# Ends of sub-layers in an encoder trunk: normalisation by quarters, three bank pairs for the transposes, and a first unit whose low part GpSimd makes

## The reference

```
for i in range(DEPTH):
    shift, scale, gate = _ada(c, ada_w[i, 0], ada_b[i, 0])
    h = x * (1.0 + scale) + shift
    y = _mixer_ab(h, ...) if i % 2 == 0 else _mixer_c(h, ...)
    x = _layer_norm(ALPHA * x + (1.0 + gate) * y, ln_g[i, 0], ln_b[i, 0])
    shift, scale, gate = _ada(c, ada_w[i, 1], ada_b[i, 1])
    h = x * (1.0 + scale) + shift
    y = _swiglu(h, ffn_w_in[i], ffn_w_out[i])
    x = _layer_norm(ALPHA * x + (1.0 + gate) * y, ln_g[i, 1], ln_b[i, 1])
```

## Time and profile before

| what | value |
|---|---|
| median of 3 runs (lowest, highest) | 2828.54 us (2824.93, 2829.81) |
| the profiled execution: its own time, its span | 2825.97 us, 2824.2 us |
| PE, DVE, ACT, POOL busy | 93%, 70%, 41%, 10% of the span |
| L477, the low parts of weights on DVE | 396 instructions, 2324 ns each |
| L472, the high parts on ACT | 396 instructions, 1915 ns each |
| L845, the power on GpSimd | 4 instructions, 947 ns each |
| mean granted clock of TensorE | 0.977 |

### The profile page before, as it was taken

The page is one execution under the profiler, slowest core; times in us unless marked ns, Lnnn a source line. Parts: engine busy times, 40 slices in busy tenths (PEclk is TensorE's granted clock), DMA queues, the critical chain, the costliest instruction groups (busy, mean ns, idle before and its releaser), DMA issues. The chain is left out here.

```text
span 2824.2 us, 42978 instructions
## 1 busy us (share of the span) xinstructions
PE 2636.7 (93%) x18094; PEld 2195.5 (78%) x18094; DVE 1973.2 (70%) x1838; ACT 1148.6 (41%) x1319; POOL 282.9 (10%) x199
## 2 busy tenths in 40 slices
PE   1999979998999999999999779999999999999996
PEld 1788869997777888888888567888778888888885
DVE  6778946776666888888887776765568755555557
ACT  1443336555434333333333335456343333333332
POOL 0000000000005000000000085541050000000000
PEclk9999979999999999999999899999999999999998
DMA  9899912220647888888887375654558755555552
GB/s 351 325 345 369 373 50 71 71 68 32 225 151 266 328 305 325 308 324 309 309 323 293 100 258 194 239 166 145 196 187 325 277 194 188 186 190 193 192 187 82
DMA packets 252881, 636.60 MB, mean 225 GB/s; under 512 B 10222, under 2 KB 17060, under 8 KB 230596
## 3 DMA queue, kind: packets, MB, share of 16 engines
q1 hardware_dynamic: 246578, 621.84, 61.4%
q10 hardware_dynamic: 6162, 12.72, 1.2%
HBM read 632.42 MB, written 2.10 MB: 225 GB/s over the span
## 5 line engine op out<-in xcount | busy, mean ns | idle before, releaser
L477 DVE TENSOR_TENSOR s_wl<-s_raw,s_wh 128x2048 fp32r<-128x2048 f32 x396 | 920.4, 2324 | 503.0 <-ACT s_wh L472 502.4
L472 ACT ACTIVATE s_wh<-s_raw 128x2048 fp32r<-128x2048 f32 x396 | 758.5, 1915 | 1168.4 <-PE pa L623 521.2
L621 PE MATMUL pa<-s_wh,s_hth 128*128 128x512 f32 x1616 | 644.5, 399 | 14.9 <-DVE s_wl L477 9.3
L622 PE MATMUL pa<-s_wl,s_hth 128*128 128x512 f32 x1616 | 633.9, 392 | 0.0
L623 PE MATMUL pa<-s_wh,s_htl 128*128 128x512 f32 x1616 | 633.8, 392 | 0.0
L621 PEld LDWEIGHTS pa<-s_wh,s_hth 128*128 128x128 f32 x1616 | 306.8, 190 | 88.8 <-issue 18.2
L623 PEld LDWEIGHTS pa<-s_wh,s_htl 128*128 128x128 f32 x1616 | 306.2, 189 | 65.5
L517 DVE SCALAR_TENSOR_TENSOR s_wide<-s_adaw,s_silu_c,s_wide 128x2048 f32<-128x2048 f32 x150 | 351.9, 2346 | 6.3 <-DMA s_adaw<-in_ada_w 6.3
L622 PEld LDWEIGHTS pa<-s_wl,s_hth 128*128 128x128 f32 x1616 | 306.9, 190 | 60.6
L621 PE MATMUL pb<-s_wh,s_hth 128*128 128x512 f32 (+1 forms) x816 | 319.1, 391 | 0.0
L622 PE MATMUL pb<-s_wl,s_hth 128*128 128x512 f32 (+1 forms) x816 | 318.5, 390 | 0.0
(11 more groups left out here) (361 smaller groups left out, 2562.1 us busy)
## 6 DMA issues: line engine op xcount, KB each, us to landing
s_raw<-in_ffn_w_in SPq DMA_DIRECT2D x176, 1024.0 KB, 5.2
s_adaw<-in_ada_w SPq DMA_DIRECT2D x160, 1024.0 KB, 6.3
s_raw<-in_ffn_w_out SPq DMA_DIRECT2D x88, 1024.0 KB, 7.4
s_raw<-in_ab_w_in SPq DMA_DIRECT2D x48, 1024.0 KB, 9.0
s_raw<-in_diff_w_in SPq DMA_DIRECT2D x48, 1024.0 KB, 5.1
s_raw<-in_ada_w SPq DMA_DIRECT2D x16, 1024.0 KB, 8.5
s_raw<-in_ab_w_out SPq DMA_DIRECT2D x16, 1024.0 KB, 5.5
s_qkv<-in_ada_w SPq DMA_DIRECT2D x16, 1024.0 KB, 7.3
```

The costliest lines, as they stand in the source:

```text
L472: act.activation(wh[:, s % 2, :, 0:width], raw[:, s, :, 0:width], ACT.Copy).then_inc(hi_done, 1)
L477: dve.tensor_tensor(wl[:, s % 2, :, 0:width], raw[:, s, :, 0:width], wh[:, s % 2, :, 0:width].bitcast(F32), ALU.subtract).then_inc(lo_done, 1)
L621: pe.matmul(o, a_hi, w_hi, start=start and k == 0, stop=False)
L622: pe.matmul(o, a_hi, w_lo, start=False, stop=False)
```

## The change

It has five parts, all in the three calls 1, 2 and 3.

1. `normal` works on a quarter of the columns (512) instead of a half (1024): quarters 0 and 1 before group 0, and 2 and 3 behind `lower(3)`.
2. The transposes use three bank pairs (`py`, `pb`, `pt`), so a group waits for the one three before it. Group 3 is moved from in front of unit 0 to between its first 12 and its second 12 matmuls (`mid`).
3. The units wait for their input group by group: k = 0 and 1 for the first of the two groups, k = 2 and 3 for the second.
4. The low part of unit 0's weights is made by GpSimd in two halves of 1024 columns (`low_first`), one in front of the power and one behind it; the first unit waits for these (`lo_first`) in place of `lo_done`. DVE no longer makes it, and raises `lo_done` for it behind `normal(3)`.
5. ACT no longer waits for `scaled(0)` before its first read of group 0.

```diff
+        def low_first(pool, c, half):
+
+            k = slice(2 * half, 2 * half + 2)
+            pool.wait_ge(hi_done, c * 4 + 1)
+            pool.tensor_tensor(wl[:, 0, k], raw[:, 0, k], wh[:, 0, k].bitcast(F32), ALU.subtract).then_inc(lo_first, 1)
...
-            pe.wait_ge(lo_done, c * 4 + s + 5)
+            if first is None:
+                pe.wait_ge(lo_done, c * 4 + s + 5)
...
+                    if first is not None and i == 0 and k % 2 == 0:
+                        pe.wait_ge(lo_first, first - 1 + k // 2)
+                    if groups is not None and i == 0 and k % 2 == 0:
+                        pe.wait_ge(h_lo, groups + k // 2 + 1)
...
+                if i == 0 and mid is not None:
+                    mid()
...
-        def turn_bank(g):
-            return (py, pb)[g % 2]
+        def turn_bank(call, g):
+            return (py, pb, pt)[g % 3] if call else (py, pb)[g % 2]
...
-                if n >= 2:
-                    pe.wait_ge(h_scaled, n - 1)
-                    pe.wait_ge(h_hi, n - 1)
-                if call and g % 4 == 0:
-                    pe.wait_ge(x_ready, 2 * call - 1 + g // 4)
+                deep = 3 if call else 2
+                if g >= deep:
+                    pe.wait_ge(h_scaled, n + 1 - deep)
+                    pe.wait_ge(h_hi, n + 1 - deep)
+                if call and g % 2 == 0:
+                    pe.wait_ge(x_ready, 4 * (call - 1) + g // 2 + 1)
...
-            turn_pe(pe, call, range(0, 4))
+            turn_pe(pe, call, range(0, 3))
...
+                    mid=lambda s: turn_pe(pe, call, range(3, 4)) if s == 0 else None)
...
-                if g == groups[0]:
+                if call == 0 and g == groups[0]:
                     act.wait_ge(h_scaled, n + 1)
...
-                cols = slice(half * D // 2, (half + 1) * D // 2)
+                cols = slice(q * W, (q + 1) * W)
...
             if call:
                 normal(0)
+                normal(1)
             two_groups(0)
-            low(dve, c, 0)
+            if not call:
+                low(dve, c, 0)
             two_groups(2)
             if call:
-                normal(1)
+                normal(2)
+                normal(3)
+                dve.wait_ge(lo_first, 2 * call)
+                dve.sem_inc(lo_done, 1)
             low(dve, c, 1)
...
+        def end_norm(pool, n, c=None):
+
+            if c is not None:
+                low_first(pool, c, 0)
             pool.wait_ge(end_var, n + 1)
             pool.tensor_tensor(small[:, 38:40], small[:, 34:36], small[:, 95:96].to_broadcast((P, NT)),
                                ALU.pow).then_inc(end_rstd, 1)
+            if c is not None:
+                low_first(pool, c, 1)
...
-            end_norm(pool, 0)
+            end_norm(pool, 0, C_FFN0)
```

More of the change, by code:

```diff
@@ L402, in build_trunk @@
         gate_out = sem("gate_out")
+        lo_first = sem("lo_first")
         end_var = sem("end_var")
@@ L608, in multiply @@
         def multiply(pe, c, s, lhs, bank, width=W, start=True, stop=True, tile0=None, k0=None,
-                     free=None):
-            pe.wait_ge(lo_done, c * 4 + s + 5)
+                     free=None, groups=None, mid=None, first=None):
+            if first is None:
+                pe.wait_ge(lo_done, c * 4 + s + 5)
             hi, lo = lhs
@@ L625, in multiply, with project @@
                     mm.then_inc(tile0, 1)
+                if i == 0 and mid is not None:
+                    mid()
             mm.then_inc(unit_done, 1)
-        def project(pe, c, n, lhs, done, free, bank, width=W, call=None, between=None, ready=None):
+        def project(pe, c, n, lhs, done, free, bank, width=W, call=None, between=None, ready=None, mid=None):
             for s in range(4):
-                if call is not None:
-                    pe.wait_ge(h_lo, 8 * call + 2 * s + 2)
                 if ready is not None:
@@ L636, in project @@
                 multiply(pe, c, s, lhs, bank, width, start=(s == 0), stop=(s == 3), tile0=done if s == 3 else None,
-                         free=(free, n) if s == 0 else None)
+                         free=(free, n) if s == 0 else None, groups=None if call is None else 8 * call + 2 * s, first=None if s or not call else 2 * call,
+                         mid=None if mid is None else lambda s=s: mid(s))
                 if between is not None:
                     between(s)
-        def turn_bank(g):
-            return (py, pb)[g % 2]
+        def turn_bank(call, g):
+            return (py, pb, pt)[g % 3] if call else (py, pb)[g % 2]
         def back_bank(c):
@@ L650, in turn_pe @@
                 n = call * 8 + g
-                if n >= 2:
-                    pe.wait_ge(h_scaled, n - 1)
-                    pe.wait_ge(h_hi, n - 1)
-                if call and g % 4 == 0:
-                    pe.wait_ge(x_ready, 2 * call - 1 + g // 4)
+                deep = 3 if call else 2
[4 more added lines that the diff above has]
+                    pe.wait_ge(x_ready, 4 * (call - 1) + g // 2 + 1)
                 for j in range(2):
                     for i in range(NT):
-                        mm = pe.transpose(turn_bank(g)[:, j, i * P:(i + 1) * P],
+                        mm = pe.transpose(turn_bank(call, g)[:, j, i * P:(i + 1) * P],
                                           xt[:, i, (2 * g + j) * P:(2 * g + j + 1) * P], ident)
@@ L662, in turn_project @@
         def turn_project(pe, call, c, n):
-            turn_pe(pe, call, range(0, 4))
+            turn_pe(pe, call, range(0, 3))
             project(pe, c, n, (hth, htl), pa_done, pa_free, pa, call=call,
-                    between=lambda s: turn_pe(pe, call, range(4 + 2 * s, 6 + 2 * s)) if s < 2 else None)
+                    between=lambda s: turn_pe(pe, call, range(4 + 2 * s, 6 + 2 * s)) if s < 2 else None,
+                    mid=lambda s: turn_pe(pe, call, range(3, 4)) if s == 0 else None)
         def turn_act(act, call, c, groups=range(0, 8)):
@@ L677, in turn_act @@
                     act.wait_ge(h_lo, n - 1)
-                src = turn_bank(g)[:, 1, 0:SEQ]
+                src = turn_bank(call, g)[:, 1, 0:SEQ]
                 act.activation(htmp[:, g % 2, 1], src, ACT.Identity, scale=small[:, k:k + 1], bias=shift[:, k:k + 1])
@@ L708, in turn_dve, with normal @@
             shift = small[:, 16:32] if call else ada[:, 0, 0:16]
-            def normal(half):
-                if half == 0:
+            def normal(q):
+                if q == 0:
                     dve.wait_ge(end_rstd, call)
-                cols = slice(half * D // 2, (half + 1) * D // 2)
+                cols = slice(q * W, (q + 1) * W)
                 for i in range(NT):
@@ L723, in scaled @@
                     dve.wait_ge(h_lo, call * 8 + g - 1)
-                dve.tensor_scalar(htmp[:, g % 2, 0], turn_bank(g)[:, 0, 0:SEQ], small[:, k:k + 1], shift[:, k:k + 1],
+                dve.tensor_scalar(htmp[:, g % 2, 0], turn_bank(call, g)[:, 0, 0:SEQ], small[:, k:k + 1], shift[:, k:k + 1],
                                   ALU.mult, ALU.add).then_inc(h_scaled, 1)
@@ L840, in end_dve @@
                 factors_dve(dve, n + 1)
-        def end_norm(pool, n):
+        def end_norm(pool, n, c=None):
+            if c is not None:
+                low_first(pool, c, 0)
             pool.wait_ge(end_var, n + 1)
@@ L1245, in _ @@
                 gla_norm(h)
-            end_norm(pool, 0)
+            end_norm(pool, 0, C_FFN0)
             end_pool(pool, 0)
             pool.memset(ysum[:], 0.0).then_inc(ysum_zero, 1)
-            end_norm(pool, 1)
+            end_norm(pool, 1, C_DIFF)
             end_pool(pool, 1)
@@ L1277, in _ @@
                 norm(m)
-            end_norm(pool, 2)
+            end_norm(pool, 2, C_FFN1)
             end_pool(pool, 2)
@@ L1621, in _ @@
             turn_act(act, 2, C_DIFF)
-            act.wait_ge(x_ready, 4)
+            act.wait_ge(x_ready, 8)
             act.dma_start(A_lam[0:1, 0:256], diff_lambda.rearrange("a b n -> a (b n)")).then_inc(lam_in, 16)
```

## The result

The changed kernel takes 2831.28 us (median of 22 runs, 2825.91 to 2834.61), the kernel before 2827.81 (22 runs, 2823.22 to 2830.41). The profiled execution has a span of 2826.1 us, 1.9 more than before.

What follows compares the result with a forecast made beforehand. TensorE's matmuls bound the kernel, except stretches from normal(0) to unit 3 in calls 1 to 3. Holds of 9.1 minus a chain gain of 4.1 make it 5.0 us slower: 2833.5 us from the median, range 2823.5 to 2839.5.

Steps and rivals of the forecast that it cites:

- The two mechanisms: In calls 1 to 3: a chain from normal(0) to unit 3 shorter by 4.1 us, and GpSimd holding DVE for 9.1.
- the holds: GpSimd's halves block DVE for whole instructions, delaying normal(0) by 2.2, 4.34 and 2.56 us, 9.1 together.
- the late group 3: Group 3, behind unit 0's first 12 matmuls, keeps DVE in scaled(3) and delays unit 1; it takes the rest of 4.5 us.
- the gain of the chain: normal(0) to unit 3 gets shorter by 1.36, 1.17 and 1.59 us in calls 1 to 3, 4.1 in all.
- a clock that the prediction did not have right: Clock rises about 4.5 us after unit 0's start, so its first 12 matmuls take 4.85 us, bounds 2.72 and 5.12.
- The chain up to unit 0: From unhindered normal(0), quarters, transposes and ACT's dropped wait start unit 0 at 4.45 us instead of 8.96.
- the first half's hold: GpSimd's half ahead of the power delays DVE: hidden in call 1, 2.14 us in call 2, 0.36 in call 3.
- The rival of shared bandwidth: GpSimd's 1024 columns take about 1 us from DVE, not 2.2; sum about nothing; no chance of its own given.
- Behind unit 0: From unhindered normal(0): group 3 at 9.3 us, unit 1 at 16.15, groups 6 and 7 at 21.6, unit 3 at 29.4.
- Rival (b): Clock falls between units 0 and 1, costing unit 1 2.1 us a call, 6.4 in all; 2839.9 us; chance 0.13.
- a change of the clock elsewhere: Sign of being wrong: the clock changes at places other than the forecast assumed; no size given.

Runs made afterwards that it cites:

- run 5: Changed kernel with GpSimd subtracting only 16 columns a half (output wrong) and group 3 transposed ahead of unit 0: 2812.61 us, ratio 0.9947 to the kernel before.
- run 2: Changed kernel with group 3 transposed ahead of unit 0 again, all else kept: 2819.74 us, ratio 0.9979 to the kernel before.
- run 8: Changed kernel with each of GpSimd's halves cut into four instructions of 256 columns: 2832.67 us, ratio 1.0013 to the kernel before.
- run 4: Changed kernel with both of GpSimd's halves ahead of the power, group 3 still late: 2829.85 us, ratio 1.0014 to the kernel before.
- run 1: Changed kernel with GpSimd's halves on 16 columns each (output wrong), group 3 still late: 2826.77 us, ratio 0.9998 to the kernel before.
- run 3: Run 2 with DVE instead of GpSimd making unit 0's low part, in one piece behind normal(1): 2815.30 us, ratio 0.9959 to the kernel before.
- 7: Changed kernel with DVE making unit 0's low part behind lower(1) as before, group 3 still late: 2835.92 us, ratio 1.0034 to the kernel before.

## Why the prediction was right

**The two mechanisms and the sign.** The prediction had a chain that becomes 4.1 us shorter and holds of 9.1 us, 5.0 slower; the time is 3.5 us slower in the medians. Both mechanisms are shown, each by a run that removes it: the holds by run 5 against run 2 (9 us) and by L709's 2.21 us for 16 columns, the late group 3 by run 2 (10 us against the changed kernel, with what the clock did as part of it). That the sum came so close is in part luck: the holds came out 0.8 smaller than said, and the gain of the chain hangs on a clock that the prediction did not have right, as follows.

**The chain up to unit 0.** Said: quarters at 1.0 and 1.9, transposes at 1.15, unit 0 at 4.45. Measured: transposes at 1.06, unit 0 at 4.41 in the changed order wherever nothing held DVE.

**GpSimd.** Said: 2.4 us for 1024 columns from rows for 256 and 512, 2.2 of hold each. Measured: 2.34 to 2.40, and holds of 2.0. Where the first half's hold falls came out too: hidden in call 1, 2.0 where 2.14 was said in call 2, 0.33 where 0.36 was said in call 3. The rival of shared bandwidth is out, by L709's 2.21 us. The Trainium skill, "SBUF — State Buffer", section "Who interferes with whom", states that the one who starts first has the shared pair for the whole instruction. The halves agree, by L709 and by the turns of run 8; the power does not, as L709 ran for its 0.17 us beside it in call 2.

**Behind unit 0.** Said: group 3 at 9.3, unit 1 at 16.15, unit 3 at 29.4. Measured without the hold: unit 3 at 28.8 to 29.0. This is the term that was mis-sized, the gain of the chain: 5.6 us in the profiled execution against 4.1. In call 1 the clock had risen before unit 0, so group 3 came at 7.2, and the fall at unit 1 took 1.6 of that back; in calls 2 and 3 the first 12 matmuls took 4.6 us and not 4.85; and the last stretch, group 6 to unit 3, took 7.6 and not 7.8. The gain is no fixed number. With group 3 late and nothing held, unit 1 starts at +14.0 where the clock rises about 4.3 us behind normal(0) (call 1 of the changed kernel, call 2 of run 4) and at +16.4 to 16.8 where it rises at about 10 (run 1, and calls 1 and 3 of run 4); in the profile of run 1 unit 3 stands at +31.3, 31.3 and 31.5, later than before. With group 3 first, a rise at 3.9 or at 8.3 leaves unit 1 at +13.9 (calls 1 and 2 of run 3). From the medians, 8.3 of holds and 3.5 slower, an estimate of the changed kernel's usual gain is 4.8.

**Rival (b)** had 0.13 and was more than that. The clock fell at unit 1 in one of three calls of the changed kernel's profile, and in all three of runs 1, 4, 7 and 8: 13 of 15 calls with group 3 late. In the 21 calls of the runs with group 3 first it never did. The prediction had named a change of the clock elsewhere among the signs of being wrong, and that sign came. A fall costs 1.6 us (7.2 instead of 5.6 from unit 1 to group 6), where 2.1 were said. That the fall and the late rise hid part of run 1's gain is argued from one profiled execution each; run 5 shows only that without the pause the gain is whole. How often the changed kernel has the fall in its 22 runs stays open. What is on record is each run's mean granted clock: 0.979 in its four fastest (up to 2827.74 us), 0.977 in the profiled one, 0.975 or 0.976 in the thirteen slowest (from 2831.19 us on). So its time goes with the clock, but where in the kernel the slower ones lost it was not seen.

## What to carry to other kernels

Work that is given to GpSimd is not off DVE's path when both use SBUF. Count each large GpSimd instruction (here 256 to 1024 columns) as a hold on the next DVE instruction that has two SBUF inputs or is a tensor_scalar from SBUF to SBUF, for up to the rest of its length (here 2.0 of 2.34 us), and look at what that instruction is on the path of. When a stall is taken away by starting the consumer early, follow what was moved behind the consumer: here a group moved behind 12 matmuls held an in-order queue with two normalisations and the next weights in it. DVE's in-order queue could do the work itself in a slot where it waited anyway, and another order of the same work was worth 17.5 us here. And a forecast that crosses a change of the clock needs both ends: the same order gave unit 1 at +14.0 or +16.8.

## What the runs showed of the hardware

A DVE instruction of 16 columns was held for 2.0 us by one GpSimd instruction in SBUF, while the small power (2 columns, 0.72 us) in SBUF held nothing. TensorE's clock rose 4.3 us behind normal(0) in call 1 of the changed kernel, before the first matmul of unit 0 and behind its transposes, but only behind matmuls of unit 0 in calls 2 and 3. And with group 3 late it fell at the start of unit 1 (0.4 us before to 0.6 behind), after a pause of 3.4 us between the units that had eight transposes in it (1.1 us), in 13 of 15 calls, and it was at 0.50 for unit 1's first matmuls although TensorE was then busy without a pause. In the other two calls, 2 and 3 of the changed kernel, the same pause brought no fall.
